# Semaphores of the first expert product raised earlier, and an altered order of decays, reciprocals and low parts in the SSD stage, in a hybrid decoder layer

## The reference

```python
n = rms_norm(h, norm_mix_w)
c_b, c_c, c_x, z, xbc, dt_raw = split(n @ w_in)
y_conv = grouped_rms_norm(c_b * dwconv3(c_c * c_x), conv_norm_w, 8)
xs, bs, cs = split(silu(dwconv4(xbc)))
y_ssd = ssd_chunked(xs * dt, dt * a, bs, cs) + ssd_d * xs     # 16 heads, 4 groups, chunks of 128
y_ssd = grouped_rms_norm(y_ssd * silu(z), ssd_norm_w, 4)
h = h + concat(y_conv, y_ssd) @ w_out
h = h + moe(rms_norm(h, norm_ffn_w))                          # top 4 of 32, clamped SwiGLU, biases
out = rms_norm(h, norm_final_w)[meta tokens dropped]
```

## Time and profile before

| | |
|---|---|
| median of three runs | 1582.28 us |
| profiled execution | 1586.74 us, span 1585.1 us |
| PE busy | 1531.7 us, 97% |
| PEld, DVE | 1000.5 us (63%), 584.9 us (37%) |
| POOL, ACT | 330.5 us (21%), 228.5 us (14%) |
| experts, first product to last | about 502 to 1545 us |

### The profile page before, as it was taken

One profiled execution on the slowest core, in us unless ns is written; L12 is line 12 of the kernel. 1 busy time (PEld: TensorE's weight loads), 2 busy tenths in 40 slices (PEclk: granted clock), 3 DMA queues, 4 the chain that ended last, 5 costly groups with the idle time before them and its releaser, 6 DMA issues.

```text
span 1585.1 us, 37739 instructions
## 1 busy us (share of the span) xinstructions
PE 1531.7 (97%) x15275; PEld 1000.5 (63%) x15275; DVE 584.9 (37%) x1221; ACT 228.5 (14%) x316; POOL 330.5 (21%) x512
## 2 busy tenths in 40 slices
PE   9999999999996999999999999999999999999996
PEld 7998899774442455655654665666556566666562
DVE  6777988862134321122211321122211321122225
ACT  4533443240021000000000000000000000000001
POOL 1000000000024232223322232223322232223320
PEclk9999999999998999999999999999999999999998
DMA  4232222334254999999999999999999999999936
GB/s 148 81 125 86 88 77 104 159 143 166 89 192 160 380 399 406 403 410 405 398 407 401 407 403 398 408 407 404 400 405 407 408 404 399 407 413 404 396 121 271
DMA packets 80788, 479.09 MB, mean 302 GB/s; under 512 B 17410, under 2 KB 18058, under 8 KB 26610
## 3 DMA queue, kind: packets, MB, share of 16 engines
q1 hardware_dynamic: 66354, 461.24, 73.0%
q0 software_dynamic: 14400, 17.37, 3.1%
HBM read 470.03 MB, written 17.01 MB: 307 GB/s over the span
## 4 chain that ended last, share of the span: by engine, by line
PE 92%; DVE 5%; issue 1%; DMA 1%; ACT 1%; POOLq 0%; SPq 0%; DVEq 0%; POOL 0%; ACTq 0%
PE bank L1660 65%; PE bank L1344 15%; PE bank L1530 7%; DMA moe_f<-in_b_gate_up 1%; PE bank L1363 1%; PE bank L1472 0%; PE bank L1475 0%; DVE w_lo L874 0%; PE bank L1473 0%; PE bank L1502 0%; DVE reg_tq L964 0%; DVE reg_tq L890 0%; PE bank L1487 0%; DVE reg_vcs L869 0%; PE bank L1721 0%
## 5 line engine op out<-in xcount | busy, mean ns | idle before, releaser
L1660 PE MATMUL bank<-ring,moe_f 128*32 128x512 f32 (+1 forms) x12240 | 1023.7, 486 | 21.9 <-DVEq L1264 10.1
L1660 PEld LDWEIGHTS bank<-ring,moe_f 128*32 128x32 f32 x12240 | 620.1, 110 | 425.0 <-issue 261.5
L1275 DVE STREAM_TRANSPOSE moe_f<-bank 128x768 f32<-128x768 f32 x32 | 31.4, 983 | 617.5 <-PE bank L1660 617.5
L1344 PE MATMUL bank<-n_hi,w_hi 128*128 128x258 f32 (+2 forms) x608 | 190.8, 314 | 7.2 <-DVE w_lo L874 4.9
L573 POOL DMA_INDIRECT moe_f<-n_scratch,idx_next x99 | 103.7, 1047 | 450.8 <-DVE moe_f L1256 415.3
L1344 PE MATMUL bank<-n_lo,w_hi 128*128 128x258 f32 (+2 forms) x608 | 187.1, 308 | 0.0
L1344 PE MATMUL bank<-n_hi,w_lo 128*128 128x258 f32 (+2 forms) x608 | 187.0, 308 | 0.0
L824 ACT ACTIVATE moe_f<-moe_f 128x768 f32<-128x768 f32 x32 | 27.1, 845 | 718.1 <-DVE moe_f L1279 718.1
L1344 PEld LDWEIGHTS bank<-n_hi,w_hi 128*128 128x128 f32 x608 | 115.0, 189 | 16.2 <-DVE w_lo L874 5.4
L580 POOL DMA_INDIRECT expert_rows<-moe_f,idx_now x96 | 98.5, 1026 | 104.5 <-ACT moe_f L830 82.9
L1344 PEld LDWEIGHTS bank<-n_lo,w_hi 128*128 128x128 f32 x608 | 115.0, 189 | 6.5 <-issue 1.2
(11 more groups left out here) (249 smaller groups left out, 806.5 us busy)
## 6 DMA issues: line engine op xcount, KB each, us to landing
ring<-in_moe SPq DMA_DIRECT2D x382, 1024.0 KB, 7.4
ring<-in_w_in SPq DMA_DIRECT2D x24, 1024.0 KB, 4.8
ring<-in_w_out SPq DMA_DIRECT2D x10, 1024.0 KB, 4.9
ring<-expert_rows SPq DMA_DIRECT2D x8, 1024.0 KB, 12.1
ring<-acs_scratch SPq DMA_DIRECT2D x4, 1024.0 KB, 7.6
idx_raw<-slot_table POOLq DMA_DIRECT2D x140, 0.8 KB
reg_vcs<-in_xT SPq DMA_DIRECT2D x4, 528.0 KB, 6.0
reg_x<-in_xrow SPq DMA_DIRECT2D x4, 512.0 KB, 6.1
```

The source lines that it names most:

```text
L1275: v.transpose(glu.rearrange("p b (g r) -> p g b r", g=GRANULES), gate).then_inc(gate_raw, 1)
L1344: ins = mm(out, w[:, n % 2, c * P:(c + 1) * P], x[:, c, first:first + width], start=c == 0 and m == 0, stop=c == KC - 1 and m == 2)
L1660: ins = mm(out[l * LANE:(l + 1) * LANE, g * width:(g + 1) * width], x[:, at, g * LANE:(g + 1) * LANE], w[:, l * width:(l + 1) * width], st ...
```

## The change: a new order, and three counters raised earlier

No arithmetic is added or removed. In the order of the program:

- Chunk step 0 (`third=False`) makes the copy of the decays and the scaled C (`scaled_c`) before masking C·B; the other chunk steps keep their order. ACT takes both exponentials before it copies B, in all four.
- At the end of each step DVE scales the first head's sums out of their bank before it makes the low part for tile 1, where it did so after.
- z tile 0 goes to bank 1 and not to bank 0, and PE no longer waits for bank 0 there. The low part of z tile 2 is made between the two reciprocals of the last `head_norms`, and no longer after the first product of y and z. The weights of the router and `stack` are prepared after the z tiles and not before them.
- DVE raises `xT_ready`, `gu_free` and `act_ready` right behind the instructions that write `x0T`. SP loads piece 1 of expert 1 as soon as `h2` is complete, ahead of the last store of normed rows. POOL clears `xg` behind its last scatter.

```diff
@@ SP queue, MoE start @@
             for m in range(TT):
+                if m == TT - 1:
+                    sp.wait_ge(h2_ready, TT)
+                    sp.dma_start(extra[1][:, :], moe_d[1, 1]).then_inc(extra_in[1], 16)
                 sp.wait_ge(n2_ready, m + 1)
...
             for m in range(2):
                 sp.wait_ge(n2_out[m], 16 * TT // 2)
-            sp.wait_ge(h2_ready, TT)
-            for q in range(2):
-                sp.dma_start(extra[q][:, :], moe_d[1, q]).then_inc(extra_in[q], 16)
+            sp.dma_start(extra[0][:, :], moe_d[1, 0]).then_inc(extra_in[0], 16)
             sp.dma_start(bias, bgu_d).then_inc(bias_in, 16)
@@ GpSimd, slot table @@
             for m in range(TT):
-                if m == TT - 1:
-                    pool.wait_ge(wout_used, 12)
-                    steps.done(g.memset(xg, 0.0))
                 pool.wait_ge(pos_ready, m + 1)
...
+            pool.wait_ge(wout_used, 12)
+            steps.done(g.memset(xg, 0.0))
             steps.settled()
             pool.wait_ge(table_out, 16 * TT * TOPK)
@@ ScalarE, SSD chunk @@
                 a.activation(score, score, ACT.Exp).then_inc(score_exp, 1)
+                a.activation(acs_b, acs_b, ACT.Exp).then_inc(e_ready, 1)
                 act.wait_ge(tok_done, i * 3 + 2 + 2)
-
                 a.copy(b_tok.rearrange("p g n -> p (g n)"), bank[:, 6, :]).then_inc(b_ready, 1)
-                a.activation(acs_b, acs_b, ACT.Exp).then_inc(e_ready, 1)
@@ ScalarE, z tiles @@
-                a.activation(z_sb[:, k % 2, :], pair(k, 0, SEQ), ACT.Silu).then_inc(free[k % 2], 1)
+                a.activation(z_sb[:, k % 2, :], pair(k, int(k == 0), SEQ), ACT.Silu).then_inc(free[k % 2], 1)
@@ VectorE, head_norms @@
-            def head_norms(i, gated=None):
+            def head_norms(i, gated=None, between=None):
...
                 for t in range(2):
                     steps.done(v.reciprocal(sqb[:, t, 0:SEQ], sqb[:, t, 0:SEQ]))
+                    if t == 0 and between is not None:
+                        between()
@@ VectorE, chunk_step @@
+                def scaled_c():
+
+                    dve.wait_ge(e_ready, i + 1)
+                    steps.done(v.tensor_copy(dec[:, :], acs_b[:, :, P - 1]))
+                    e4 = acs_b.rearrange("p (g r) l -> p g r l", g=GROUPS)
+                    dve.wait_ge(chunk_ready, i + 1)
+                    steps.settled()
+                    v.tensor_tensor(e4, e4, chunk[:, 12:16, :].unsqueeze(2).to_broadcast([P, GROUPS, PER_GROUP, P]), ALU.mult
+                                    ).then_inc(cs_ready, 1)
+
+                if not third:
+                    scaled_c()
                 dve.wait_ge(tok_done, i * 3 + 2 + 3)
...
-                dve.wait_ge(e_ready, i + 1)
...
+                if third:
+                    scaled_c()
...
                 gate_conv(5, 1)
-                split(1, halved(7), 1, 0)
-
                 for t in range(2):
                     dve.wait_ge(tile_done, used(6 + t))
                     v.tensor_scalar(sqb[:, t, 0:SEQ], pair(t, 0, SEQ), 1.0 / P, EPS, ALU.mult, ALU.add
                                     ).then_inc(free[t], 1)
+                    if t == 0:
+                        split(1, halved(7), 1, 0)
@@ VectorE, after the chunks @@
-            head_norms(TT)
+            def split_z(n):
+                s, t = Z_AT[n]
+                split(n, WT_C + n + 1, s, t)
+
+            head_norms(TT, between=lambda: split_z(2))
...
                 v.tensor_tensor(y_ssd[:, k, :], y_ssd[:, k, :], z_sb[:, k % 2, :], ALU.mult).then_inc(yz_ready, 1)
-                if k + 2 < KC:
-                    s, t = Z_AT[k + 2]
-                    split(k + 2, WT_C + k + 3, s, t)
+                if 0 < k < KC - 2:
+                    split_z(k + 2)
@@ VectorE, MoE start @@
+            dve.sem_inc(xT_ready, 1)
+            dve.sem_inc(gu_free, 1)
+            dve.sem_inc(act_ready, 1)
             gated(3)
             steps.settled()
...
-            dve.sem_inc(gu_free, 1)
-            dve.sem_inc(act_ready, 1)
             dve.wait_ge(bias_in, 16)
             up_bias = bias.rearrange("p (n k b) -> p n k b", k=2, b=FF_BLOCKS)[:, :, 1, :]
             v.tensor_scalar(up_bias, up_bias, 1.0, None, ALU.add).then_inc(bias_ready, 1)
-            dve.sem_inc(xT_ready, 1)
@@ TensorE, z tiles @@
                 pe.wait_ge(wl_ready, WT_C + k + 1)
-                pe.wait_ge(free[k % 2], FREE_C + k // 2)
+                if k:
+                    pe.wait_ge(free[k % 2], FREE_C + k // 2)
                 for c in range(KC):
                     if k == 0 and c == 4:
                         head_squares(TT - 1, 1)
-                    ins = mm3(pair(k, 0, SEQ), k, c, META, SEQ)
+                    ins = mm3(pair(k, int(k == 0), SEQ), k, c, META, SEQ)
```

More of the change, by code:

```diff
@@ L1079, in group_norm @@
                                            sq[:, 0, 0:SEQ], ALU.mult, ALU.mult).then_inc(ys_ready, 1)
+            dve.wait_ge(y_free, TT)
+            for k in range(KC):
+                if k == 4:
+                    group_norm(0)
+                if k == 6:
+                    group_norm(1)
+                dve.wait_ge(free[k % 2], FREE_C + k // 2 + 1)
+                v.tensor_tensor(y_ssd[:, k, :], y_ssd[:, k, :], z_sb[:, k % 2, :], ALU.mult).then_inc(yz_ready, 1)
+                if 0 < k < KC - 2:
+                    split_z(k + 2)
+            group_norm(2)
+            group_norm(3)
             dve.wait_ge(router_in, 32)
```

16 lines of the change are left out of this document (removed).

## The result

The changed kernel takes 1572.33 us (median of 4 runs, 1571.30 to 1573.33), the one before 1583.05 us on the same chip (4 runs, 1581.72 to 1585.86). The ratio is 0.9930, 95% interval 0.9913 to 0.9947: 10.7 us faster, where I forecast 18.7 (1563.6 us, range 1560.5 to 1569.0). The direction was right, the size was not, and the time lies above my range.

A forecast was written before the change was run, and what follows sets the result against it. PE, busy 97% of the span, was taken as the bound, so only its idle time and slow stretches could be won. Gains of 2.05 + 7.1 + 9.6 = 18.7 us off 1582.3 gave 1563.6 us, range 1560.5 to 1569.0.

The forecast's parts named there:

- rival 3: SSD stage: the new order only moves waits, PE loses 9.1 us again, only the experts gain: 1572.7 us; chance 0.05.
- The bound: Expert stage: weights wait for PE, so starting PE earlier there should end the kernel earlier by as much.
- Chunk 0: Before the products of y in chunk 0: DVE's reordered work fills its idle time and PE's wait goes, gain 2.05 us.
- The first z tiles: SSD stage, z tiles 0 to 3: shorter waits and no slow clock, less a new wait at tile 3, gain 7.1 us.
- Start of the experts: First two expert products: PE starts when x0T is written, and the second product starts 9.6 us earlier.
- When does the gather land?: Start of the experts: estimated that the gathered rows land at 514.0, between 511.6 and 515.2, setting the second product's start.
- the third term: Start of the experts: the second product starts at 516.9, a gain of 9.6 us, bounds 8.4 and 11.0.
- that leaves 2.6 us less in front: Before the list read: one weight load goes ahead of the store of rows, so the chain to the gather starts 2.6 us sooner.
- the list is half covered: Reading the block list before the gather: SP's earlier weight loads overlap half of it, adding 0.5 us.
- the gather wholly: Gather of rows for the second product: SP's earlier weight loads overlap all of it, adding 1.9 us.
- rival 2: First expert product or PE's wait for the gather: the clock falls all the same, costing 1.5 us, 1565.1 us; chance 0.10.
- Rivals 1: Start of the experts: weights hold the gather longer, the third gain falls to 4.4 us, time 1568.8 us; chance 0.14.

The follow-up runs named there:

- a_third: The changed kernel with no further edit, measured again beside its variants on one chip: 1571.83 us, ratio 0.9919 to the kernel before.
- e3_again: The changed kernel with SP holding all ring loads of the expert stage until the gathered rows are in: 1564.20 us, ratio 0.9866 to the kernel before.
- c_again: The changed kernel with both early pieces behind the stores, DVE's bank transposes ahead of the gathered rows, and SP pausing after two ring loads: 1567.82 us, ratio 0.9890.
- after: The changed kernel with no further edit, in its first measurement and profile: 1572.33 us, ratio 0.9930 to the kernel before.
- a_after_again: The changed kernel with no further edit, run again on a chip of the faster sort: 1536.40 us, ratio 0.9925 to the kernel before.

## Why the prediction was wrong, point by point

The time alone would fit rival 3 (1572.7 us against the measured 1572.33): the gain of the SSD stage lost again, and that of the experts whole. That is chance. The runs show the reverse, as the terms below do one by one.

**The bound.** "What starts PE earlier there should end the kernel earlier by as much" holds on the chips for which I said it (sort P), and not on Q. My evidence for it was weak: SP waits 680.8 us for PE in the changed kernel on P and still 552.5 us on Q, where the stream paces the last blocks. The time from issue to landing, and the spacing of the blocks over the stage, tell the two apart.

**Chunk 0**: right. PE goes on at 145.32, the time I gave, and the gain is 2.05 us.

**The first z tiles**: right. Tile 3 starts at 318.15, where my times less the 2.05 give 318.55, and waits 0.79 us for 0.8. The clock stays at 1.00. Over the stage, `x0T` is written 491.82 - 481.86 = 9.96 us earlier for a forecast of 9.15, and the order alone gave 10.3 us.

**Start of the experts**: the raised counter does start PE with `x0T`, in 0.06 us. Wrong is the step "When does the gather land?", and with it the third term: forecast 9.6 us with bounds of 8.4 and 11.0, measured 4.3 less 1.7 for the clock, 2.6. The prediction's own sign of being wrong, a gather more than 21.5 us after `x0T`, is there. By its links, against the end of `x0T`, where I had the gather at 21.2 us and it came at 26.5:
- "that leaves 2.6 us less in front": nothing. The clearing and the wait behind it are 0.75 + 5.11 = 5.86 us from the last scatter's issue, and 5.90 before, with half the weights under way. Short by 2.6.
- "the list is half covered": 5.45 us where I took 3.63 + 0.5. By the loaded row, 5.32, it was covered whole. Short by 1.3.
- "the gather wholly": 6.0 us where I took 4.5. Short by 1.5. The row I used, 4.4 us beside a stream, was no upper bound.

That is 5.4 us. The rest is rival 2: PE stood 8.5 us and not 1.4, and the clock fell, 1.7 us. Rivals 1 and 2 are no alternatives; the one brings the other, and I had them as two cases with chances of their own. Together they give 18.7 - 5.4 - 1.7 + 0.8 (the stage before was better) = 12.4 us, inside the measured 8.4 to 13.8 and beside the 12.9 us of `a_third`.

The Trainium skill, "DMA: Bandwidth & Descriptors", section "Issuing engines are not separate DMA queues", says that transfers from all engines' queues run on the same DMA engines. The trace agrees: list and gather take 5.45 and 6.0 us beside SP's loads and 3.02 and 1.8 us without them. I had put the loads beside the gather at 1.4 us (11.0 less 9.6). Holding them back was worth 7.6 us (`e3_again` against `a_third`). They do not explain all of the 5.4 us above: the first link, 2.6 us, is the scatters' own time, 5.2 us or more in every run.

**The moved load**: I counted that the biases and the block list come earlier as no cost. It lets SP's loads start sooner into the list and the gather (by 1.6 us on Q, 2.7 on P), and costs 2.7 us on Q. On P the medians are as far apart, but the ranges of runs overlap, and in the two traces the second product starts only 0.7 us sooner with the load late, so for P this is not shown.

## What to carry to other kernels

A start that comes earlier also sends earlier what stands behind it. Before you count its gain, ask which small transfers on the path (a list, a gather) the large ones now fall beside, and take the worst row under load for them, not the mean. Hold back a prefetch until such a transfer is in, if the buffers last that long: that was worth 7.6 us here where PE paces the stage, and nothing where the stream does. A delay that makes TensorE's wait longer costs the wait and the fall of the clock behind it together: they are one case, not two. And when one wait has been made shorter, look again at what comes last: an order of DVE that helped a little while the gather was late held PE up once it was not.

## What the runs showed of the hardware

- Where I looked, behind idle times of PE of 1.5 to 2.2 us the granted clock stayed at 1.00, behind those of 3.8 us and more it was 0.5 (1.2 GHz) for the next 3 to 6 us: in `e3_again` 1.00 from 506.94 to 510.94, in `a_third` 0.50 from 511.28 to 515.28. From its first matmul to its 49th the second product takes 5.15 us at the full clock (`e3_again`), 7.41 in `a_third` and 8.11 in `c_again`, so a cut of the idle time from 7.0 to 3.8 us won nothing of it back.
- The time from the last scatter's issue until it counted as landed was 5.2 to 6.7 us in every run, with 1 or 2 MB of weights in flight. The list read took 1.8 to 5.7 us and the gather 1.8 to 6.0, the long ones with weight loads beside them.
- The same kernel takes 1549 us on some chips and 1584 on others, at the same granted clock. The gate-up product takes 20.69 us on both; the down product takes 10.27 us on the one sort and 11.4 to 11.7 on the other. One thing more differs: PE's weight loads in the experts take 110 ns each on both, but together they cover 621.0 us of the trace of `after` (P) and 404.2 us of that of `a_after_again` (Q), so on P the loads lie less on top of each other. What slows the matmuls of 256 columns stays open.
